# Squares as the moving operand: the sums behind 21 norms of a two-block transformer kernel

## The reference

```python
def layer_norm(x, g, b):
    mu = jnp.mean(x, -1, keepdims=True)
    var = jnp.mean(jnp.square(x - mu), -1, keepdims=True)
    return (x - mu) * lax.rsqrt(var + LN_EPS) * g + b

def rmsnorm(z, g):
    return z * lax.rsqrt(jnp.mean(z * z, -1, keepdims=True) + EPS) * g

# first block, each of two layers
x = layer_norm(ALPHA * x + gm_x * mix_x, ln_g[layer, 0], ln_b[layer, 0])
x = layer_norm(ALPHA * x + gf_x * swiglu(x * (1.0 + scf_x) + shf_x, w_in, w_out), ln_g[layer, 1], ln_b[layer, 1])
# second block, each of three parts
h = rmsnorm(x, g_pre) * (1 + scale) + shift
x = x + w * gate * rmsnorm(part(h), g_post)
```

## Time and profile before

| | before |
|---|---|
| median of 3 runs | 3950.0 us (3945.5 to 3950.17) |
| the profiled execution | 3940.2 us, its span 3938.3 us |
| TensorE busy | 3730.9 us, 95% |
| VectorE busy | 1944.4 us, 49% |
| ScalarE busy | 1543.3 us, 39% |
| GpSimd busy | 1330.9 us, 34% |
| mean granted clock of TensorE | 0.984 |

### The profile page before, as it was taken

How to read it: one execution, slowest core, us unless ns; L and a number is a source line. 1 busy time by engine, 2 the same in 40 slices (tenths; PEclk the granted TensorE clock), 3 DMA queues, 4 the chain that set the end, 5 groups by cost and what they waited for, 6 DMA issues and landing times.

```text
span 3938.3 us, 52901 instructions
## 1 busy us (share of the span) xinstructions
PE 3730.9 (95%) x21907; PEld 3152.6 (80%) x21907; DVE 1944.4 (49%) x2968; ACT 1543.3 (39%) x2460; POOL 1330.9 (34%) x837
## 2 busy tenths in 40 slices
PE   7999989999999999998999999999989989999999
PEld 5877667889987677676888889999877777788887
DVE  4455566444356666766212354445458745432123
ACT  4133445333235433424422453333355527443223
POOL 2010003334343424426232434434434424353224
PEclk9999999999999999999999999999999999999999
DMA  5221123333332121124333432222422211242333
GB/s 185 74 84 33 44 91 127 99 102 107 97 115 88 33 63 50 38 59 139 106 103 102 134 107 67 68 67 71 153 74 65 59 39 41 70 143 83 98 97 108
DMA packets 463226, 342.99 MB, mean 87 GB/s; under 512 B 18073, under 2 KB 433803, under 8 KB 462987
## 3 DMA queue, kind: packets, MB, share of 16 engines
q1 hardware_dynamic: 462304, 339.35, 28.4%
q10 hardware_dynamic: 683, 0.26, 0.0%
HBM read 334.32 MB, written 5.24 MB: 86 GB/s over the span
## 4 chain that ended last, share of the span: by engine, by line
PE 77%; DVE 9%; ACT 5%; POOL 3%; DMA 3%; issue 2%; SPq 0%; ACTq 0%; POOLq 0%; DVEq 0%
PE PS L107 76%; DVE A L124 2%; PE PS L115 2%; ACT A L118 1%; POOL RWr L124 1%; POOL TM L124 1%; DVE A L132 1%; ACT L118 1%; ACT RWH L121 1%; DMA MW<-in_w_ada 1%; DMA MW<-in_mod_w 1%; DVE RWr L124 1%; DVE SM L144 1%; DVE TM L132 1%; DVE XT L124 1%
## 5 line engine op out<-in xcount | busy, mean ns | idle before, releaser
L124 POOL TENSOR_TENSOR RWr<-RW,RWH 128x1024 fp32r<-128x1024 f32 (+2 forms) x304 | 685.1, 2256 | 1590.7 <-ACT RWH L121 1584.6
L107 PE MATMUL PS<-HTH,RWH 128*128 128x512 f32 (+2 forms) x2688 | 989.2, 368 | 26.7 <-DVE HTr L124 8.6
L107 PE MATMUL PS<-HTr,RWH 128*128 128x512 f32 (+2 forms) x2688 | 956.4, 356 | 0.0
L107 PE MATMUL PS<-Ar,RWH 128*128 128x256 f32 (+2 forms) x3584 | 906.6, 343 | 20.2 <-DVE Ar L124 7.5
L107 PE MATMUL PS<-HTH,RWr 128*128 128x512 f32 (+3 forms) x2528 | 903.0, 357 | 0.0
L107 PEld LDWEIGHTS PS<-Ar,RWH 128*128 128x128 f32 x3584 | 622.8, 191 | 114.2 <-issue 21.8
L107 PE MATMUL PS<-Ar,RWr 128*128 128x256 f32 (+2 forms) x1792 | 607.3, 339 | 0.0
L107 PEld LDWEIGHTS PS<-HTH,RWH 128*128 128x128 f32 x2688 | 511.9, 190 | 118.1 <-issue 34.9
L121 ACT ACTIVATE RWH<-RW 128x1024 fp32r<-128x1024 f32 (+2 forms) x478 | 474.1, 999 | 319.2 <-DMA RW<-in_ffn_w_out 135.1
L107 PEld LDWEIGHTS PS<-HTr,RWH 128*128 128x128 f32 x2688 | 512.5, 191 | 64.1 <-issue 6.5
L107 PEld LDWEIGHTS PS<-HTH,RWr 128*128 128x128 f32 (+1 forms) x2528 | 481.3, 190 | 64.1 <-issue 0.2
(11 more groups left out here) (211 smaller groups left out, 4782.4 us busy)
## 6 DMA issues: line engine op xcount, KB each, us to landing
RW<-in_ffn_w_in SPq DMA_DIRECT2D x176, 512.0 KB, 3.8
MW<-in_mod_w SPq DMA_DIRECT2D x83, 512.0 KB, 4.0
MW<-in_w_ada SPq DMA_DIRECT2D x72, 512.0 KB, 4.4
RW<-in_ffn_w_out SPq DMA_DIRECT2D x80, 384.0 KB, 3.5
RW<-in_ffn_w_out SPq DMA_DIRECT2D x52, 512.0 KB, 3.8
RW<-in_mix_w_in SPq DMA_DIRECT2D x41, 512.0 KB, 3.8
RW<-in_ssd_w_in SPq DMA_DIRECT2D x40, 512.0 KB, 3.9
RW<-in_ev_w_in SPq DMA_DIRECT2D x24, 512.0 KB, 3.9
```

What stands on the lines that cost most here:

```text
L107: return self._ins(self.real and self.real.matmul(o, l, r, start=start, stop=stop, skip_group_check=True))
L124: return self._ins(self.real and self.real.tensor_tensor(out=o, in0=i0, in1=i1, op=op))
```

## The change

The operands of the `var` step are exchanged. 32 columns of `k.mean` (all 1/1024) are loaded and 128 tokens of squares move. The output is 32 equal rows of 128 sums, and the tokens 128x to 128x + 127 go to the partitions 32x to 32x + 31, so four groups of tokens fill a bank's 128 partitions by 128 columns (two groups 64 partitions). The scale of 1/1024 is in the loaded operand. Root and reciprocal then work on 128 (or 64) partitions by 128 columns, in a new tile `root` for each of the two places of sums. In the spread the loaded operand is a column of the identity that picks row 32x, broadcast to 128 columns, and the tile of reciprocals moves; with two groups the contraction is over 64 rows. Steps, their order, semaphores and banks stay as they are.

```diff
         for x in range(n // 128):
-            last = p.mm(k.banks.of("var", *key)[:, x:x + 1], sq.bufs[slot][:, 128 * x:128 * x + 128], k.ones[:, 0:1],
-                        i == 0 and x == 0, i == 4)
+            last = p.mm(k.banks.of("var", *key)[32 * x:32 * x + 32, 0:128], k.mean[:, 0:32],
+                        sq.bufs[slot][:, 128 * x:128 * x + 128], i == 0, i == 4)
...
-        m, sq = (part[1] - part[0]) // 128, k.sums[part[3]]
+        rows, sq = (part[1] - part[0]) // 4, k.sums[part[3]]
...
-        s.act(sq.st[:, 0:m], k.banks.of("var", *key)[:, 0:m], ACT.Sqrt, bias=k.epsc, scale=1.0 / D).then_inc(
+        s.act(k.root[part[3]][0:rows, :], k.banks.of("var", *key)[0:rows, 0:128], ACT.Sqrt, bias=k.epsc[0:rows, :]).then_inc(
             "s.root", *key).frees("var", *key)
...
-        m, sq = (part[1] - part[0]) // 128, k.sums[part[3]]
+        rows, st = (part[1] - part[0]) // 4, k.root[part[3]]
         v.wait_ge("s.root", *key)
-        v.rcp(sq.st[:, 0:m], sq.st[:, 0:m]).then_inc("v.rstd", *key)
+        v.rcp(st[0:rows, :], st[0:rows, :]).then_inc("v.rstd", *key)
...
-            last = p.mm(pv[:, 128 * x:128 * x + 128], sq.st[:, x:x + 1].to_broadcast([128, 128]), k.ident, True, True)
+            last = p.mm(pv[:, 128 * x:128 * x + 128], k.ident[0:32 * m, 32 * x:32 * x + 1].to_broadcast([32 * m, 128]),
+                        st[0:32 * m, :], True, True)
...
+        k.root = [sb(f"root{i}", [128, 128]) for i in range(2)]
```

More of the change, by code:

```diff
@@ L797, in root_vector @@
     def root_vector(v, k, key, part):
-        m, sq = (part[1] - part[0]) // 128, k.sums[part[3]]
+        rows, st = (part[1] - part[0]) // 4, k.root[part[3]]
         v.wait_ge("s.root", *key)
-        v.rcp(sq.st[:, 0:m], sq.st[:, 0:m]).then_inc("v.rstd", *key)
+        v.rcp(st[0:rows, :], st[0:rows, :]).then_inc("v.rstd", *key)
     @staticmethod
     def root_tensor(p, k, key, part):
-        m, sq = (part[1] - part[0]) // 128, k.sums[part[3]]
+        m, st = (part[1] - part[0]) // 128, k.root[part[3]]
         pv = k.banks.take(p, 1, "rstd", *key)
```

## The result

The changed kernel takes 3925.0 us (3920.5 to 3930.2, four runs) against 3947.8 us for the kernel before, measured beside it: a ratio of 0.9943, 95% interval 0.9927 to 0.9959, or 22.7 us faster. On another chip it was 3931.9 against 3948.7 us, 0.9958 (0.9944 to 0.9972), 16.8 us. So it is faster by about 0.5%, where 0.3% was forecast.

What follows compares the result with a forecast made beforehand. TensorE, busy 3730.9 of 3938.3 us, was taken as the bound, with waits second. The terms -17.1 - 4.4 + 5.1 + 3.4 + 1.0 - 6.8 + 6.5 give -12.3 us from 3950.0, so 3938 us, range 3921 to 3955.

Steps and rivals of the forecast that it cites:

- the clock rival: Rival for the whole kernel: 14 us gained from TensorE's clock, 15% of the queue gain lost, 3927 us; chance 0.14.
- Part 1, the sums: The 105 var steps on TensorE: 17.1 us gained, plus 4.4 us where a modulation row follows the burst.
- Groups in turn: Rival at the sums: the column groups run one after another, +26 us, 3976 us; chance 0.03.
- Part 2, the spread: The 17 spreads of 256 tokens contract over 64 rows; changing form costs 0.30 us each, 5.1 us lost.
- The ceiling of 0.33: At the 64-row spread: entering and leaving that form costs at most 0.33 us, as for columns.
- Part 3, root and reciprocal: Between last sum and spread: chain 0.89 us longer, 21 times, mostly hidden; 3.4 us lost plus 1 us in VectorE's queue.
- the covers: TensorE work between last sum and spread hides the longer chain: more than 0.89 us left in 14 parts, less in seven.
- root chain on the path: Rival between last sum and spread: the longer chain is exposed in all parts, +18 us, 3968 us; chance 0.10.
- Part 4, the clock: TensorE around the long bursts at 2800 and 609: two low-clock stretches avoided, 6.8 us gained.
- What survives: TensorE's queue: of 21.5 us saved, 30% is lost to other waits, 6.5 us (bounds 10% and 75%).
- The signs: Changed profile: named burst, spread, root and reciprocal times; wrong if low clock appears elsewhere or waits grow over 7 us.
- Absorbed: Rival for the whole kernel: sums get shorter but the next wait takes it, +4 us, 3954 us; chance 0.25.

Runs made afterwards that it cites:

- the narrow root: The changed kernel with root and reciprocal on 2 of the 128 columns, norms not computed: 3919.5 us, 0.9924 of the kernel before.
- the twins: The changed kernel with one extra matmul per sum, moving one column (4077.1 us, 1.0323) or 128 columns (4060.4 us, 1.0289); norms not computed.

## Why the prediction came out as it did

The sign was right and both times lie in the range: 12.3 us were forecast, 22.7 and 16.8 came. The first of them, 3925.0 us, is nearer to the clock rival's 3927 than to the forecast's 3938. The prices of the sums, the root and the reciprocal were right, the chain behind them was counted too cheap, and the other terms together gave more than was forecast. That the total came out inside the range is in part luck.

**Part 1, the sums.** Right in each price: 0.54 us for a burst of one step (0.53), 0.22 for each further one ((1.19 - 0.53) / 3 = 0.22), 1.2 us for p0's four steps (1.21), and two steps with a modulation row 0.54 + 0.22 + 0.76 - 0.33 = 1.19 (1.19). Groups in turn, a rival, is out. The modulation rows and the 8-column matmuls of the earlier trace rows had shown all that was needed.

**Part 2, the spread.** The mechanism was right, the size short: 0.39 us for each, 6.6 us of TensorE's queue in all, against 0.30 and 5.1. Of these 6.6 us the time gave back 2.1, not clear of noise, when the form was taken out. The ceiling of 0.33 was taken from the narrow form; going into and out of the 64-row form costs more in this stream.

**Part 3, root and reciprocal.** The durations were right (0.36 and 0.945 us for 0.37 and 0.95), and in the kernel before their effect would have been about right too (4.7 us measured with the wide reciprocal there). The step that failed is the one that carried the covers over: "In 14 parts more of it is left over at the reciprocal's end than 0.89 us" was read where TensorE ran slowly and where other engines came early. Around the root of the norm p0 stands, in the kernel before:

```profile
2802.45 1.28 ACT L118 ACT_TABLE_LOAD   x1
...
2804.58 0.26 ACT L118 ACTIVATE SM<-PS,cols 128x4 f32<-128x4 f32 x1 [0.85 <-PE PS L107]
...
2808.39 1.91 PE L107 MATMUL PS<-CC,SM 128*128 128x128 f32 x8
```

And in the changed kernel, ScalarE, VectorE and TensorE:

```profile
2805.43 0.42 ACT L118 ACTIVATE TM<-XT 128x256 f32<-128x256 f32 x1 [1.35 <-DVE XT L124]
2805.87 1.28 ACT L118 ACT_TABLE_LOAD   x1
2807.16 0.37 ACT L118 ACTIVATE root<-PS,cols 128x128 f32<-128x128 f32 x1
...
2807.56 0.95 DVE L138 RECIPROCAL root<-root 128x128 f32<-128x128 f32 x1 [2.16 <-ACT root L118]
...
2808.66 1.13 PE L107 MATMUL PS<-root,CC 128*128 128x128 f32 x8 [1.20 <-DVE root L138]
```

The last sum starts before 2805.04, but the root starts at 2807.16: ScalarE has a square and the table load still to do, which the burst of 3.9 us had hidden. In the kernel before the root waited for TensorE there, and started at 2804.58. Behind it, 3.3 us of matmuls at 1.2 GHz covered the reciprocal; at 2.4 GHz they are done at 2807.46, and TensorE waits 1.20 us. The second kind is Pre b1, H0, in the changed kernel:

```profile
2281.23 2.56 DVE L124 TENSOR_TENSOR RWr<-RW,RWH 128x1024 fp32r<-128x1024 f32 x1 [13.62 <-ACT RWH L121]
...
2281.89 0.36 ACT L118 ACTIVATE root<-PS,cols 64x128 f32<-64x128 f32 x1 [0.69 <-PE PS L107]
...
2283.71 0.93 DVE L138 RECIPROCAL root<-root 64x128 f32<-64x128 f32 x1
...
2284.79 0.68 PE L107 MATMUL PS<-root,CC 64*128 64x128 f32 x4 [2.11 <-DVE root L138]
```

The root is done at 2282.25, but VectorE is in a weight half until 2283.7. Of the rival root chain on the path the mechanism has come true in nine or ten norms of 21, where seven were counted, and with larger waits (9.3 and 7.4 us in the two profiles, for 4.6). The whole price of the width in the changed kernel is 12.4 us by the medians against 4.4 predicted (3.4 and 1); the low end of its band, 5 us, is still above that.

**Part 4, the clock.** The mechanism was right, and it is shown: with 128 moving columns in place of one, and records, root, reciprocal and spread as they were, the low stretches behind the long bursts go, and the time falls by 18.6 us (13 to 24). What failed is "there are two that nothing but the bursts explains": only the long bursts were counted. These alone give about 4 us (0 to 7.5) for the 6.8 that they were put at.

For the changed kernel itself the clock's share is smaller than these 18.6 us. Its mean clock rose by 0.004 (0.981 to 0.985), that of the kernel with 128 columns of ones by 0.007 on the same chip. What 0.001 of clock is worth can be estimated: 18.6 us for 0.007 are 2.5 us, the runs of one kernel among themselves also give about 2.5 us (1.8 to 2.5 for the kernel before on three chips), and the twins, 16.6 us for 0.012, give 1.4. By this estimate 6 to 10 of the 16.8 us are clock, against 6.8 forecast and within the bound of 14, and 7 to 11 us come from all the rest, against 5.5 forecast. Likewise 3 to 5.5 of the 12.4 us for the narrow root would be clock (0.985 to 0.987), and the others are near the 5.5 to 7.4 us by which TensorE waits less for the reciprocal. Why the changed kernel keeps less clock than the one with wide ones was not tried.

**What survives.** The 30% was not tested by an experiment. Of the two profiles of the changed kernel the second has the clock of the profile before, 0.984: TensorE is busy 20.8 us less and waits 12.5 us more, and 6.3 us of these are the reciprocal (7.4 + 0.7 against 1.8). The other 6.2 us are 30% of 20.8; the first profile gives 11.0 of 29.3, 38%. This is one execution against another and includes clock, so it supports the size and does not show it. Nor do the differences between kernels settle it. Taken as a sum, 16.8 us less 6 to 10 of clock, with the width (7 to 9 without its clock) and the spread (2.1) added back, leave some 16 to 22 us for the sums, where 15 net and 21.5 gross were forecast; but such terms need not add.

**The signs.** The prices of burst, root and reciprocal came as named, the low clock behind p0's burst went, and the spread adds 0.83 us where 0.7 was named. One sign said that the prediction is wrong if waits grow by more than 7 us: they grew by 19.2 and 12.5 us. By its own sum (3.4 + 1.0 + 6.5) they were to grow by 10.9, so the sign was set too low, and the waits for the chain were still underrated. The sign of low clock at new places can't be read from single profiles. From 52 to 60 us, in code that is the same in all kernels, the clock is 1.00 in the profile before and 0.58 and 0.79 in the two of the changed kernel; from 116 to 124 us it is 1.00 before and 0.79 in the changed kernel, and also 0.79 in the kernel before with the wide reciprocal.

**Absorbed and the clock gives more.** The clock rival named 14 us of clock and 3927 us; the time came near it in the first measurement (3925.0), but its 14 us of clock are more than the 6 to 10 estimated here, so its number is not a proof of it. Absorbed is out as a total, since both measurements are clearly faster, though in the profiles 19 of 29 and 12.5 of 20.8 us of TensorE's time did turn into waits.

## What to carry to other kernels

Where a matmul with one moving column costs as much as one with 128 (0.112 us a record here), let 128 columns move: it cost nothing more, and the clock rose from 0.981 to 0.988. Exchanging the operands and using column groups is cheap for many tokens or several steps in a row (32 records in 1.2 us for 3.6), dear for a lone short one (0.53 us for 0.45), and it widens what follows: price the root, the reciprocal and the form of the next matmul with it. Covers read from a trace hold for its clock and its order of arrivals only; take the cover as matmuls at full clock, and look for what else stands ahead of the chain in the other engines' queues. And compare clocks over several runs: profiles of one kernel differ in where the low stretches lie.

## What the runs showed of the hardware that was not expected

TensorE can be full by its busy time and lose its clock. 32 records with one moving column in 3.9 us have a granted clock of 0.89 inside and 0.50 behind, and 0.55 behind in a second kernel with the same burst; the same records with 128 moving columns have 1.00. The Trainium skill (TensorE: Matmul & The Clock Gate, Part 1) lets the clock depend on how busy TensorE has been. The trace agrees with the two levels, but by busy time alone it does not: both bursts are 100% busy.

Alternating between the narrow and the full form costs about 0.5 us for each pair of fp32 matmuls (128.5 us for 250), and the 64-row form 0.39 us for going in and out. A reciprocal takes 0.945 us for 128 columns, 6.2 ns a column, on 64 partitions as on 128 (931 to 952 ns in all 21).
